# VectorE instead of three DMAs makes the threefold weight sum in six feed-forward quarters

## What is computed

```python
# first block                      (x, h: 512 x 1024; w_ff_in: 1024 x 4096; w_ff_out: 4096 x 1024)
ff = jnp.einsum('bsf,fd->bsd',
                jnp.square(jax.nn.relu(jnp.einsum('bsd,df->bsf', h, w_ff_in[l]))),
                w_ff_out[l])
x = layer_norm(DEEPNORM_ALPHA * x + (1.0 + g2) * ff, ln2_g[l], ln2_b[l])
...
# second block
f = jnp.square(jax.nn.relu(jnp.einsum('bsd,df->bsf', h2, w_mlp1[l])))
x = x + jnp.einsum('bsf,fd->bsd', f, w_mlp2[l])
```

## Time and profile before

| what | us |
|---|---|
| median of 3 runs | 1379.66 |
| the three runs | 1377.70, 1379.66, 1379.86 |
| the profiled execution | 1377.24 |
| its span | 1375.5 |
| TensorE busy | 1324.8 (96%) |
| VectorE busy | 836.8 (61%) |
| GpSimd busy | 623.4 (45%) |
| mean granted TensorE clock | 0.995 |

### The profile page before, as it was taken

One profiled execution on the slowest core, in us unless ns is written; L12 is line 12 of the kernel. 1 busy time (PEld: TensorE's weight loads), 2 busy tenths in 40 slices (PEclk: granted clock), 3 DMA queues, 4 the chain that ended last, 5 costly groups with the idle time before them and its releaser, 6 DMA issues.

```text
span 1375.5 us, 16594 instructions
## 1 busy us (share of the span) xinstructions
PE 1324.8 (96%) x6471; PEld 1090.6 (79%) x6471; DVE 836.8 (61%) x1151; ACT 657.6 (48%) x919; POOL 623.4 (45%) x503
## 2 busy tenths in 40 slices
PE   2999999999999999999999996999999999999999
PEld 2888778888878888888888875887788888888887
DVE  6586987789861677708158396648722661906337
ACT  0645445466774165445353455424535544545353
POOL 0453855433335856251443505673744535153440
PEclk9999999999999999999999998999999999999999
DMA  9343534755324525867769543225133686766953
GB/s 341 114 109 124 118 123 147 207 157 172 116 64 154 165 82 127 219 161 151 229 126 254 129 104 122 92 92 128 52 99 124 142 225 150 165 203 153 244 122 92
DMA packets 149837, 202.93 MB, mean 148 GB/s; under 512 B 10140, under 2 KB 94384, under 8 KB 148480
## 3 DMA queue, kind: packets, MB, share of 16 engines
q1 hardware_dynamic: 123760, 146.95, 34.0%
q0 software_dynamic: 19760, 49.53, 17.7%
q10 hardware_dynamic: 6240, 5.40, 1.6%
HBM read 189.12 MB, written 2.26 MB: 139 GB/s over the span
## 4 chain that ended last, share of the span: by engine, by line
PE 87%; DVE 7%; POOL 2%; ACT 1%; issue 1%; DMA 1%; SPq 0%; ACTq 0%; DVEq 0%; POOLq 0%
PE bank L2098 26%; PE bank L2100 26%; PE bank L2099 26%; DVE tmp L1642 2%; PE bank L2304 2%; POOL w_lo L686 2%; PE bank L2314 1%; DMA arena<-in_w_ada_dram 1%; PE bank L2725 1%; PE bank L2497 1%; PE bank L2289 1%; PE bank L2317 1%; PE bank L2279 1%; PE bank L2498 1%; POOL w_lo L824 1%
## 5 line engine op out<-in xcount | busy, mean ns | idle before, releaser
L686 POOL TENSOR_TENSOR w_lo<-raw,w_hi 128x512 fp32r<-128x512 f32 x180 | 260.2, 1475 | 274.4 <-ACT w_hi L937 274.4
L2098 PE MATMUL bank<-w_hi,a_hi 128*128 128x512 f32 x864 | 341.3, 395 | 9.4 <-DVE a_lo L1433 6.2
L2100 PE MATMUL bank<-w_hi,a_lo 128*128 128x512 f32 x864 | 337.9, 391 | 0.0
L2099 PE MATMUL bank<-w_lo,a_hi 128*128 128x512 f32 x864 | 337.7, 391 | 0.0
L2098 PE MATMUL bank<-a_hi,w_hi 128*128 128x512 f32 (+1 forms) x832 | 321.4, 386 | 2.7 <-DVE a_lo L1433 1.7
L2100 PE MATMUL bank<-a_hi,w_lo 128*128 128x512 f32 (+1 forms) x832 | 317.5, 382 | 0.0
L2099 PE MATMUL bank<-a_lo,w_hi 128*128 128x512 f32 (+1 forms) x832 | 317.5, 382 | 0.0
L824 POOL TENSOR_TENSOR w_lo<-raw,w_hi 128x512 fp32r<-128x512 f32 x112 | 150.9, 1452 | 180.4 <-ACT w_hi L1060 180.4
L2098 PEld LDWEIGHTS bank<-w_hi,a_hi 128*128 128x128 f32 x864 | 163.1, 189 | 47.1 <-issue 10.2
L2100 PEld LDWEIGHTS bank<-w_hi,a_lo 128*128 128x128 f32 x864 | 162.9, 189 | 34.3
L2099 PEld LDWEIGHTS bank<-w_lo,a_hi 128*128 128x128 f32 x864 | 163.2, 189 | 32.6
(11 more groups left out here) (279 smaller groups left out, 1696.1 us busy)
## 6 DMA issues: line engine op xcount, KB each, us to landing
raw<-in_w_in_dram SPq DMA_DIRECT2D x24, 1024.0 KB, 5.2
raw<-in_w_mlp_dram SPq DMA_DIRECT2D x24, 1024.0 KB, 6.0
arena<-in_w_ada_dram SPq DMA_DIRECT2D x18, 1024.0 KB, 6.6
raw<-in_w_ff_in_dram SPq DMA_DIRECT2D x16, 1024.0 KB, 7.7
arena<-in_w_ff_out_dram POOLq DMA_DIRECT2D x13, 1024.0 KB, 8.7
arena<-in_w_mlp_dram POOLq DMA_DIRECT2D x13, 1024.0 KB, 8.6
raw<-in_w_out_dram SPq DMA_DIRECT2D x12, 1024.0 KB, 5.5
raw<-in_w_in_dram SPq DMA_DIRECT2D x16, 512.0 KB, 5.4
```

Source lines behind the costliest of these rows:

```text
L686: last = pool.tensor_tensor(w_lo[:, u0 % 2, cols], raw[:, u0 % 2, cols], w_hi[:, u0 % 2, cols].bitcast(F32), ALU.subtract)
L2098: pe.matmul(out_, hi_a, hi_b, start=start, stop=False, skip_group_check=resumed)
L2099: pe.matmul(out_, hi_a, lo_b, start=False, stop=False, skip_group_check=resumed)
L2100: return pe.matmul(out_, lo_a, hi_b, start=False, stop=stop, skip_group_check=resumed)
```

## The change

In every quarter VectorE makes t2_sum with its two additions; the three DMAs of the six later quarters, their semaphore and GpSimd's waits for them are gone. The diff, cut where it only renames:

```diff
-                def t2_start(i):
-                    pool.dma_start(unit(t2_sum), down(i, 0, 0)).then_inc(t2_in, 16)
-
-                def t2_add(i, half):
-                    pool.wait_ge(t2_in, t2_copied(g0 + i) - 32 + 16 * half)
-                    pool.dma_start(unit(t2_sum), down(i, half, 1), accum_op=ALU.add).then_inc(t2_in, 16)
-
                 for i in range(QUARTERS):
                     g, u = g0 + i, u0 + FF_OPS * i
                     for n in range(2 if i == 0 else 0, OP_M2):
                         ff_lo(u0, i, n)
                         if n == 3:
-                            if i:
-                                pool.wait_ge(landed[u0 % 2], slot_landed(u0, i, 4))
-                            else:
-                                pool.wait_ge(t2_made, 2 * (g // QUARTERS) + 1)
+                            pool.wait_ge(t2_made, 2 * g + 1)
                             pool.dma_start(unit(even), down(i, 1, 1), accum_op=ALU.add).then_inc(t3_in, 16)
-                        elif n == 0:
-                            t2_add(i, 1)
                     pool.wait_ge(w_lo_made, u + OP_M1 + 1)
                     pool.dma_start(unit(b11), down(i, 0, 1), accum_op=ALU.add).then_inc(t1_in, 16)
                     pool.wait_ge(w_lo_made, u + OP_M2 + 1)
-                    if i:
-                        pool.wait_ge(t2_in, t2_copied(g))
-                    else:
-                        pool.wait_ge(t2_made, 2 * (g // QUARTERS) + 2)
+                    pool.wait_ge(t2_made, 2 * g + 2)
                     pool.dma_start(b21, t2_sum, accum_op=ALU.add).then_inc(t4_in, 16)
-                    if i < QUARTERS - 1:
-                        pool.wait_ge(t4_in, 16 * g + 16)
-                        pool.wait_ge(w_lo_made, u + OP_M6 + 1)
-                        t2_start(i + 1)
-                        t2_add(i + 1, 0)
...
-                elif n == OP_M6 and i:
-                    act.wait_ge(t2_in, t2_copied(g))
                 elif n == OP_M6:
-                    act.wait_ge(t2_made, 2 * (g // QUARTERS) + 2)
+                    act.wait_ge(t2_made, 2 * g + 2)
...
-                if i == 0:
-                    dve.wait_ge(b_landed[0], 16 * g + 16)
-                    dve.wait_ge(landed[u0 % 2], slot_landed(u0, i, 4))
-                    if g == 0:
-                        dve.wait_ge(ln_made, 4)
-                    dve.tensor_tensor(t2_sum, b11, raw[:, u0 % 2], ALU.add).then_inc(t2_made, 1)
+                dve.wait_ge(b_landed[0], 16 * g + 16)
+                dve.wait_ge(landed[u0 % 2], slot_landed(u0, i, 4))
+                if g == 0:
+                    dve.wait_ge(ln_made, 4)
+                if i:
+                    dve.wait_ge(t4_in, 16 * g)
+                    dve.wait_ge(w_lo_made, u - FF_OPS + OP_M6 + 1)
+                dve.tensor_tensor(t2_sum, b11, raw[:, u0 % 2], ALU.add).then_inc(t2_made, 1)
                 split_low(g, A11, sq[:, 0:4, 0:256], 0)
-                if i == 0:
-                    dve.wait_ge(landed[(u0 + 1) % 2], slot_landed(u0, i, 5))
-                    dve.wait_ge(t2_made, 2 * (g // QUARTERS) + 1)
-                    dve.tensor_tensor(t2_sum, t2_sum, raw[:, (u0 + 1) % 2], ALU.add).then_inc(t2_made, 1)
+                dve.wait_ge(landed[(u0 + 1) % 2], slot_landed(u0, i, 5))
+                dve.wait_ge(t2_made, 2 * g + 1)
+                dve.tensor_tensor(t2_sum, t2_sum, raw[:, (u0 + 1) % 2], ALU.add).then_inc(t2_made, 1)
```

More of the change, by code:

```diff
@@ L328, in build @@
         prod_lo, c0_lo, x_read, z_made = sem("prod_lo"), sem("c0_lo"), sem("x_read"), sem("z_made")
-        t1_in, t2_in, t3_in, t4_in, t2_made = sem("t1_in"), sem("t2_in"), sem("t3_in"), sem("t4_in"), sem("t2_made")
+        t1_in, t3_in, t4_in, t2_made = sem("t1_in"), sem("t3_in"), sem("t4_in"), sem("t2_made")
         b_landed = [sem("b11_landed"), sem("b21_landed")]
@@ L375, in slot_landed @@
             return landed_at(u0 + n % 2) + 16 * (3 * i + n // 2)
-        def t2_copied(g):
-            return 48 * (g - g // QUARTERS)
         def op_source(u0, n):
```

## The result

| | before | after |
|---|---|---|
| median of 6 runs, us | 1378.53 | 1383.70 |
| lowest to highest | 1377.13 to 1379.86 | 1382.61 to 1384.31 |
| profiled execution (span) | 1377.24 (1375.5) | 1382.61 (1380.9) |
| ratio after to before | | 1.0039, 95% interval 1.0029 to 1.0049 |
| HBM read, MB | 189.1 | 170.3 |

The changed kernel is 5.2 us slower, with 18.9 MB less read. The forecast was 6.65 us on top of a start that was taken as 1378.6, so 1385.3.

What follows compares the result with a forecast made beforehand. TensorE, busy 96% of the span, was taken as the bound. Quarter losses of 3 x 0.75 + 2 x 1.3 + 1.8 = 6.65 us on a mean of 1378.6 gave 1385.3 us, range 1381.5 to 1389.5.

Steps and rivals of the forecast that it cites:

- Removed DMAs: Taking 18 DMAs of 1 MB out of six quarters is worth 0 on the path, between 0 and 1.2 us.
- Rival 3: Faster because HBM traffic was the bound; 1374 us, chance 0.03.
- Turns between VectorE and GpSimd: Two-input VectorE additions and GpSimd reads of SBUF wait for each other, delaying units 3 and 4; an addition's turn 2.2 us.
- Rival 1: No change: quarter 4's 0.75 us belongs to its start from another stage; chance 0.15.
- Early landing: Quarters 1, 6 and 7: B12 lands 4.9 us after issue, unit 3 is just late; 0.75 us per quarter.
- Late landing: Quarters 2 and 5: B12 lands 6.3 or 6.2 us after issue, the seventh tile starts late; 1.3 us each.
- Quarter 3: B12 is fetched 21.0 us in, beside `residual`, so unit 3 ends late for the seventh tile; 1.8 us.
- Rival 2: Larger loss: both units and the M2 chain late, one after the other; 2.3 us a quarter, 1392.4 us, chance 0.09.

Runs made afterwards that it cites:

- experiment 4: Kernel before without the three DMAs of the six later quarters and with no additions in their place; 1377.42 us beside 1377.88 of the kernel before.
- experiment 1: Changed kernel with both additions of the six later quarters replaced by one-operand VectorE reductions of the same length; 1377.85 us beside 1377.88 of the kernel before.
- experiment 8: Changed kernel with the fetch of B12 held back in the six later quarters to 22.6 us into the quarter instead of 19.3; 1388.98 us.
- experiment 6: As changed kernel, but first addition moved behind unit 3's `w_lo`, B22 added by DMA, M7's DMA behind M5's; median 1375.66 us beside 1378.07 of the kernel before.
- experiment 3: Changed kernel with only the first addition of the six later quarters replaced by a one-operand VectorE reduction; 1381.65 us.
- experiment 7: Changed kernel with 44 at once fulfilled waits at the start of TensorE's code, so that instruction queue packets come earlier in the program; 1384.39 us.
- experiment 2: Changed kernel with only the second addition of the six later quarters replaced by a one-operand VectorE reduction; 1381.72 us.
- experiment 5: Changed kernel with the first addition moved behind the split of A11 and `w_lo` of unit 3, where GpSimd has nothing to read; 1385.82 us.

## Why the prediction was right, and where it was off

- **Removed DMAs worth 0:** right but for 0.12 us that the removal costs in quarter 3, shown by experiment 4; the sum's "no less than 0" did not see it. Rival 3, that traffic was the bound, falls with it.
- **Turns between VectorE and GpSimd as the way to TensorE:** right, shown by experiments 1 and 8. Rival 1, that quarter 4's price belonged to its start, falls: quarters 1, 6 and 7 pay the same 0.7, and experiment 6 takes it from quarter 4 by moving nothing but the sums.
- **Early landing, 0.75 us:** 0.72, 0.74 and 0.7 in quarters 1, 6 and 7. Quarters 6 and 7 lose it as forecast, at all three places: in quarter 6 0.15 at the seventh tile, 0.20 at M1 and 0.11 at M2, each with 0.08 at the next matmul and a little behind it. In quarter 1 the account does not hold: nothing is lost at the seventh tile, 0.50 at M1 and 0.17 at M2, and experiment 3 shows that the second addition alone makes the same loss. The sum is nearly the same because a loss at the seventh tile moves the later deadlines with it.
- **Late landing, 1.3 us:** 1.32 and 1.16 in quarters 2 and 5, all but 0.03 of it at the seventh tile as forecast. That the landing makes it is shown by 7 and 8.
- **Quarter 3, 1.8 us:** the term that was off, 1.1. The step that failed is "B12 is fetched at 764.07, 21.0 us in". In the changed kernel it is fetched 20.3 us in (766.11). `residual` and units 1 and 2 meet in other turns there: before, its second instruction waited through all four parts of unit 1 and took 6.26 us; after, the two engines alternate, and unit 2 takes 6.01 instead of 6.80.

```profile
745.98 6.26 DVE L1972 SCALAR_TENSOR_TENSOR arena<-arena 128x1024 f32<-128x1024 f32 x1
```
```profile
748.81 2.19 DVE L1947 SCALAR_TENSOR_TENSOR arena<-arena 128x1024 f32<-128x1024 f32 x1
```
```profile
746.06 2.20 DVE L1961 SCALAR_TENSOR_TENSOR arena<-arena 128x1024 f32<-128x1024 f32 x1
```
```profile
763.35 11.49 SPq L528 DMA_DIRECT2D raw<-in_w_ff_out_dram  x2
```

  The first is before, the second after; the third and fourth are experiment 4, in which only the DMAs are gone: the same 2.20 us, and B12 fetched 763.35 - 743.08 = 20.3 us in. So it is the removal that changes the turns, and not the additions. One of the DMAs stood between units 0 and 1, and without it unit 1 starts 2.3 us into the quarter instead of 2.6, with the instruction at 3.0 in both. I took the turns of a stretch in which no instruction of VectorE changes as fixed. With the fetch 20.3 us in, the prediction's own turns give about 0.9 us at the seventh tile (an estimate: the addition from 25.3, unit 3 done at 33.6, the tile due at 32.8); measured are 0.8 there, 0.15 at M2 and the 0.12 of the removal.
- **The rest of the sum:** 6.65 was forecast, 5.7 is what the quarters lost; 0.7 of the difference is quarter 3. The median moved by 5.2. That the remainder lies in the two untouched stretches is so in the profiled executions; the last section says what one of them is. They partly cancel (+0.7 and -1.2), which was not forecast: that the median lies so near the forecast is in part luck.
- **Rival 2, a larger loss by turns one after the other:** did not come, since a later deadline moves with TensorE, as quarters 1 and 2 of experiments 2 and 3 show.

## What to carry to other kernels

Work given to an engine with idle time is not free if it reads two operands from SBUF while GpSimd reads too (2.29 us of it cost 1.3 us of TensorE here, the same 2.29 us with one operand nothing): ask which of GpSimd's instructions it will meet, and what is due behind those. A term that is only a fraction of a microsecond per stage can be read in advance from the one stage that already does what the others will do. Moving one of two such instructions out of the way can let the other meet more turns; the sum is that of a queue, so redo it after every edit.

## What was not expected of the hardware

**The clock's slow stretch does not sit at a fixed place of the work.** Behind the first feed-forward TensorE waits twice, 4.7 us and, ending 8.7 us later, 6.7 us (from the start of one matmul to that of the next). Around the first wait its granted clock falls to half (1.2 of 2.4 GHz), and it comes back only behind the second. But the fall comes at a place that differs: in the kernel before at 830.94, 0.5 us after the matmul that ends the first wait (830.47); in the changed kernel at 832.36, 2.1 us ahead of it (834.44). The mean granted clock tells the same: before, 0.59 in the 5 us from 830, so full speed up to 830.9; after, 0.92 in the 10 us up to 834, so half speed for the last 1.6.

```profile
830.00:835.00 5.00, 1.77 (x8) 1.14 (x8) 4.86 (x6) 4.47 (x8) 2.36 (x2) 0.59 0.30 68
```
```profile
824.00:834.00 10.00, 6.11 (x27) 4.72 (x26) 9.59 (x19) 2.44 (x2) 4.76 (x5) 0.92 0.36 118
```

The return differs with it: the slow stretch is 13.65 us long in all ten kernels. The matmuls behind the second wait come 0.427 us apart until then, 11 of them in the kernel before, 5 in the changed one:

```profile
843.96 0.63 PE L2100 MATMUL bank<-w_hi,a_lo 128*128 128x512 f32 x1
844.39 0.49 PE L2098 MATMUL bank<-w_hi,a_hi 128*128 128x512 f32 x1
844.72 0.40 PE L2099 MATMUL bank<-w_lo,a_hi 128*128 128x512 f32 x1
```
```profile
845.38 0.63 PE L2075 MATMUL bank<-w_hi,a_lo 128*128 128x512 f32 x1
845.81 0.49 PE L2073 MATMUL bank<-w_hi,a_hi 128*128 128x512 f32 x1
846.14 0.39 PE L2074 MATMUL bank<-w_lo,a_hi 128*128 128x512 f32 x1
```

The first of these two is before, the second after. Six matmuls fewer at 0.2 us each are the 1.2 us by which the stage between is shorter. Over the kernels here the stage takes 213.0 us with 5 such matmuls (after, experiment 6), 213.4 with 7 (experiments 2 and 3), 213.6 with 8 (experiment 8) and 214.2 to 214.4 with 10 to 12 (before, experiments 1, 4, 5 and 7). None of the edits touches that stage; what sets the moment of the fall was not tried. So a single profile of this kernel has 1.2 us in it that belong to where the clock fell and not to a change.
